# Hybrid decoder block: the cross-attention value weights of the prologue by column pairs, with transposes threaded in and the third token tile's statistics moved

## The reference

```python
k = (memn @ w_xk).reshape(B, M, XATTN_HEADS, XATTN_HEAD_DIM)
v = (memn @ w_xv).reshape(B, M, XATTN_HEADS, XATTN_HEAD_DIM)
s = jnp.einsum('bshd,bmhd->bhsm', q, k).astype(jnp.float32) * (XATTN_HEAD_DIM ** -0.5)
o = jnp.einsum('bhsm,bmhd->bshd', p, v).reshape(B, S, XATTN_HEADS * XATTN_HEAD_DIM)
```

## Time and profile before

| | |
|---|---|
| runs | 3040.64, 3043.88, 3046.34 us |
| median | 3043.88 us |
| the profiled execution, its own time | 3043.22 us |
| its span (first to last instruction) | 3041.5 us |
| TensorE busy | 2956.7 us |
| VectorE, ScalarE, GpSimd busy | 1627.4, 1069.0, 1255.0 us |

### The profile page before, as it was taken

The page is one execution under the profiler, slowest core; times in us unless marked ns, Lnnn a source line. Parts: engine busy times, 40 slices in busy tenths (PEclk is TensorE's granted clock), DMA queues, the critical chain, the costliest instruction groups (busy, mean ns, idle before and its releaser), DMA issues. The chain is left out here.

```text
span 3041.5 us, 41966 instructions
## 1 busy us (share of the span) xinstructions
PE 2956.7 (97%) x14334; PEld 2449.6 (81%) x14334; DVE 1627.4 (54%) x2236; ACT 1069.0 (35%) x1975; POOL 1255.0 (41%) x1126
## 2 busy tenths in 40 slices
PE   7999999999999999999999999999999999999998
PEld 7888788878878888878888778887888788887887
DVE  2564566645366444445565456665635644444445
ACT  4522445424233333322233244542423333332212
POOL 6422454452224444454442244445221444445433
PEclk9999999999999999999999999999999999999999
DMA  6622222141112222253322232224111122225221
GB/s 231 213 94 103 91 83 70 59 169 42 61 65 77 83 83 83 83 193 112 124 98 87 103 102 72 69 66 163 56 56 70 56 83 83 83 83 193 83 111 76
DMA packets 131685, 297.39 MB, mean 98 GB/s; under 512 B 11825, under 2 KB 52849, under 8 KB 131569
## 3 DMA queue, kind: packets, MB, share of 16 engines
q1 hardware_dynamic: 69072, 226.07, 21.4%
q10 hardware_dynamic: 62496, 69.78, 6.7%
HBM read 222.37 MB, written 73.43 MB: 97 GB/s over the span
## 5 line engine op out<-in xcount | busy, mean ns | idle before, releaser
L2409 DVE TENSOR_TENSOR h<-h,PS 128x1024 f32<-128x1024 f32 x272 | 330.9, 1220 | 332.0 <-PE PS L2588 214.9
L2586 PE MATMUL PS<-act_hi,w_hi 128*128 128x512 f32 (+1 forms) x1088 | 428.5, 394 | 9.5 <-issue 5.5
L1535 DVE TENSOR_TENSOR copied<-copied,PS 128x512 f32<-128x512 f32 x308 | 207.5, 685 | 400.9 <-PE PS L2588 387.9
L2588 PE MATMUL PS<-act_hi,w_lo 128*128 128x512 f32 (+1 forms) x1088 | 406.6, 374 | 0.0
L2587 PE MATMUL PS<-act_lo,w_hi 128*128 128x512 f32 (+1 forms) x1088 | 405.6, 373 | 0.0
L2050 POOL TENSOR_TENSOR w_lo<-raw,w_hi 128x256 fp32r<-128x256 f32 (+1 forms) x144 | 193.8, 1369 | 435.0 <-ACT w_hi L2127 435.0
L611 POOL TENSOR_TENSOR part_lo<-sum_s,part_hi 128x512 fp32r<-128x512 f32 x176 | 229.7, 1307 | 229.4 <-ACT part_hi L1060 229.4
L2586 PE MATMUL PS<-down,mid 128*128 128x512 f32 x704 | 276.6, 393 | 7.3 <-DVE h L2409 7.3
L2586 PE MATMUL PS<-op_t_hi,part_hi 128*128 128x512 f32 x704 | 275.3, 391 | 0.0
L2588 PE MATMUL PS<-down,mid 128*128 128x512 f32 x704 | 274.8, 390 | 0.0
L2587 PE MATMUL PS<-op_t_lo,part_hi 128*128 128x512 f32 x704 | 274.8, 390 | 0.0
(11 more groups left out here) (331 smaller groups left out, 6097.9 us busy)
## 6 DMA issues: line engine op xcount, KB each, us to landing
raw<-in_w_units SPq DMA_DIRECT2D x156, 512.0 KB, 3.9
gu_raw<-in_w_units SPq DMA_DIRECT2D x64, 512.0 KB, 5.1
a_d<-copied SPq DMA_DIRECT2D x88, 256.0 KB, 2.2
mid_raw<-a_d SPq DMA_DIRECT2D x44, 512.0 KB, 4.1
qkvz_d<-stage ACTq DMA_DIRECT2D x64, 256.0 KB, 2.7
raw<-att_d SPq DMA_DIRECT2D x32, 512.0 KB, 3.2
h<-in_x SPq DMA_DIRECT2D x12, 1024.0 KB, 7.9
prep_raw<-in_w_units SPq DMA_DIRECT2D x16, 512.0 KB, 4.4
```

Source lines behind the costliest of these rows:

```text
L1535: dve.tensor_tensor(buf[dst][:, :], buf[a][:, :], bank(k), ALU.add)\
L2409: dve.tensor_tensor(h[:, t, :], h[:, t, :], flat(bank(b + 2 * (t % 2), 2)), ALU.add)\
L2586: nc.tensor.matmul(out_ap, whi, xhi, start=start, stop=False)
L2588: return nc.tensor.matmul(out_ap, wlo, xhi, start=False, stop=stop)
```

## The change

The last two of the eight value tiles are no longer done tile by tile but pair of column blocks by pair: for each pair both tiles are added, so v0 is complete after the first 12 of the last 48 products. T0 is issued between the third and the fourth pair. The item table is reordered to v0 v1 v2 t0 v3 t1, on TensorE, ScalarE and VectorE. The first wait of the last two tiles is now for the last weight tile. Token tile 2's statistics go from ahead of v0 to behind p0 on ScalarE, its normalising from behind k7 to behind p1 on VectorE; tile 3's statistics go from behind p0 to behind p1, its normalising from behind p1 to behind t4. GpSimd's and SP's streams are not changed.

```diff
 PREP = {n: i for i, n in enumerate(
-    ["k%d" % u for u in range(KT)] + ["v%d" % q for q in range(KT // 2)] +
-    "t0 t1 t2 t3 p0 p1 t4 t5 p2 p3 t6 t7 p4 p5 p6 p7".split() +
+    ["k%d" % u for u in range(KT)] +
+    "v0 v1 v2 t0 v3 t1 t2 t3 p0 p1 t4 t5 p2 p3 t6 t7 p4 p5 p6 p7".split() +
     ["p%d" % i for i in range(8, 16)])}
 RING = 4
+PAIRED = 2
...
-X_TILE = dict(k7=[0, 1, 2], p1=[3], t5=[4], p3=[5], t7=[6], p5=[7])
-X_STATS = dict(p0=[3], t5=[4], p2=[5], t7=[6], p4=[7])
+X_TILE = dict(k7=[0, 1], p1=[2], t4=[3], t5=[4], p3=[5], t7=[6], p5=[7])
+X_STATS = dict(p0=[2], p1=[3], t5=[4], p2=[5], t7=[6], p4=[7])
...
-            for i in range(3):
+            for i in range(2):
                 x_stats(i)
-            for q in range(KT // 2):
-                prep_hi(act, f"v{q}")
-            for u in range(4):
-                prep_hi(act, f"t{u}")
+            for name in "v0 v1 v2 t0 v3 t1 t2 t3".split():
+                prep_hi(act, name)
...
-            for k in range(KT):
+            def value_weights(k, u):
+
                 n = KT + k
-                pe.wait_ge(S["w_lo_ready"], n + 1)
+                us = slice(u * P, (u + 1) * P)
+                return three(PS[:, u, 0:N_MEM], w_hi[n % RING][:, us], w_lo[n % RING][:, us],
+                             act_hi[:, k, 0:N_MEM], act_lo[:, k, 0:N_MEM], k == 0, k == KT - 1)
+
+            for k in range(KT - PAIRED):
+                pe.wait_ge(S["w_lo_ready"], KT + k + 1)
                 for u in range(KT):
...
+                    last = value_weights(k, u)
+                last.then_inc(S["vm_full"], 1)
+            pe.wait_ge(S["w_lo_ready"], 2 * KT)
+
+            def value_pair(q):
+
+                for u in (2 * q, 2 * q + 1):
+                    for k in range(KT - PAIRED, KT):
+                        last = value_weights(k, u)
+                last.then_inc(S["pr_full"], 1)
...
-            for u in range(4):
+            for q in range(3):
+                value_pair(q)
+            prep_transposes(0)
+            value_pair(3)
+            for u in range(1, 4):
                 prep_transposes(u)
```

More of the change, by code:

```diff
@@ L2748, in _ @@
             pe.wait_ge(S["pr_lo"], KT)
-            for k in range(KT):
+            def value_weights(k, u):
                 n = KT + k
-                pe.wait_ge(S["w_lo_ready"], n + 1)
-                for u in range(KT):
[L2753 to L2759, removed]
+                us = slice(u * P, (u + 1) * P)
[3 more added lines that the diff above has]
+                pe.wait_ge(S["w_lo_ready"], KT + k + 1)
+                for u in range(KT):
+                    last = value_weights(k, u)
[6 more added lines that the diff above has]
+                last.then_inc(S["pr_full"], 1)
             def prep_transposes(u):
```

## The result

The changed kernel takes 3047.46 us in the median of 20 runs (3045.07 to 3050.12), the kernel before 3042.11 in 20 (3039.56 to 3046.34): a ratio of 1.0018 with a 95% interval of 1.0011 to 1.0025. It is 5.3 us slower; the interval leaves 1 out, so the loss is real, but with 0.18% it lies just inside the 0.2% that the prediction had drawn as its line. The profiled execution of the changed kernel took 3048.43 us, its span 3046.7, 5.2 more than before.

A forecast was written before the change was run, and what follows sets the result against it. TensorE, busy for 97% of the span, was taken as the bound. The -1.2 us gain is inside +5.0; with +1.5 for the clock, +6.5 on 3043.22 gives 3049.7, 3050.4 for the runs, range 3045.0 to 3053.5.

The forecast's parts named there:

- The mechanism: GpSimd's third chain waits behind p0, delaying masks and fourth chain; VectorE waits at tile 3, TensorE at T7 5.2 us.
- Rival B: GpSimd's masks don't matter: T7 is not held if they take under 3.9 us; only the 1.2 us gain remains; chance 0.06.
- Pairs and freed queue: Last two value tiles by pairs, tile 2 out of VectorE's way: p0 at 76.14 instead of 77.36, a 1.2 us gain.
- The last weight tile: Start of value tile 6 on TensorE: its second half, ended by GpSimd at 64.52, is needed earlier; wait about 0.06 us.
- The tables: Moved statistics and normalising of token tiles on ScalarE and VectorE: no cost of their own forecast beside the masks.
- rival C: Low clock lasts through p4 into the tile transposes, and ScalarE's queue adds some: +7.4 to +9.5 us; chance 0.18.
- The masks: GpSimd's instructions between third and fourth chain: 9.16 us, from 82.62 to 91.8, making p4 5.0 us late.
- The clock: TensorE's clock falls to the low level after the 5.2 us hole at T7: 1.5 us, between 0 and 2.4.
- Rival A: T7 waits but the clock stays up, or the masks take 8.1 us: +5.0, or +4.0 to +5.5; chance 0.34.
- VectorE's wait: VectorE idle some 7.6 us until released by GpSimd's stat_r, named as a sign that the forecast is right.

The follow-up runs named there:

- masks first: The changed kernel with GpSimd doing two chains, then the masks, then the chains of tiles 2 to 7; 3041.71 us, ratio 0.9996 to the kernel before.
- p3 twice: The changed kernel with the 24 products of p3 issued twice into the same place; 3047.11 us, ratio 1.0017 to the kernel before.
- p3 three times: The changed kernel with the products of p3 issued three times into the same place; 3046.57 us, ratio 1.0017 to the kernel before.
- masks twice: The changed kernel with GpSimd's seven masks built twice; 3054.25 us, ratio 1.0042 to the kernel before.
- two masks behind: The changed kernel with five of seven masks ahead of GpSimd's third chain, two and the small rest behind it; 3042.09 us, ratio 0.9998 to the kernel before.

## Why the prediction came out as it did

The changed kernel was forecast at 3050.4 us in a range of 3045.0 to 3053.5; it took 3047.46. Of the 2.9 us between 3050.4 and that, 1.8 lie in the kernel before, whose median over 20 runs is 3042.11 and not the 3043.88 of three; the change itself was put at +6.5 and measured +5.3. The chances were split between slower (0.50) and within 0.2% (0.46), and the measured 0.18% falls into the second, close to the line.

**The mechanism** was right as put: GpSimd's unchanged order, the third chain in front of the masks, VectorE at tile 3, T7 behind t5. It is shown three ways, by taking it away, by doubling it and by finding where it starts. Rival B is out: the masks matter. Its threshold of 3.9 us was worked out from the time at which TensorE could take T7; 4.1 turned out free, since ScalarE's statistics hold the fourth chain as long anyway. That the two lie so close is luck.

**The terms**, from V to p8, +6.34 us:

- *Pairs and freed queue:* forecast -1.2, measured -1.27 with all weights in time (masks first). "What is late next is t1's split, 1.4": it was, 1.24.
- *The last weight tile:* forecast 0.06, measured 0.7. TensorE took tile 6 at 18.06 us after V in the changed kernel and at 17.37 in the masks-first one. The term was mis-sized since the low part's end, 64.52 in one trace, was taken for a fixed time. It hangs on a load. The lines are ScalarE's high part of the fourth value tile, before the change and after it, and GpSimd's last two low parts after it:

```profile
51.53 1.06 ACT L2189 ACTIVATE w_hi<-prep_raw 128x1024 fp32r<-128x1024 f32 x1 [2.79 <-DMA prep_raw<-in_w_units]
51.96 1.06 ACT L2190 ACTIVATE w_hi<-prep_raw 128x1024 fp32r<-128x1024 f32 x1 [2.77 <-DMA prep_raw<-in_w_units]
60.19 4.78 POOL L2029 TENSOR_TENSOR w_lo<-prep_raw,w_hi 128x1024 fp32r<-128x1024 f32 x2
```

  ScalarE waits for the load of this tile, in either kernel, and starts 4.39 us after V before the change and 5.00 after it. From there GpSimd makes five low parts without a pause, 2.4 us each, up to 64.97. The change asks for the last of them one tile, 2.9 us, earlier and so used up all the slack. Nothing in the change touches that load, so the term is not a fixed price: in the four kernels with the same program up to p0 this start lies from 4.19 to 5.00 us after V, and p0 scatters by 0.8 us. What delays the load is open.
- *The tables:* forecast nothing beside the masks, measured +1.3. The prediction saw that ScalarE has one statistics more between t5 and p2 and left it to rival C; it didn't ask what VectorE waits for once the masks are gone. This part of C was true.
- *The masks:* forecast 9.16, measured 91.68 - 83.05 = 8.63. They cost 35.86 - 30.28 = 5.58 from p0 to p8 with the clock, 4.2 without it. The 0.5 us that they are shorter is the first select, 1.10 us in place of 1.67. The forecast's 5.0 for p4 was net of the pairs' gain and had the tables' price in it unseen: without the gain it is 97.33 - 76.14 - (92.35 - 77.36) = 6.2 for masks and tables, measured 4.2 + 1.3 = 5.5.
- *The clock:* forecast 1.5, measured 1.35 (p4 alone 4.68 - 3.15 = 1.53). Rival A, that it would hold, is out: the fall is in the profiled execution, and the mean granted clock of a run is 0.995 in 17 of the changed kernel's 20 and 0.996 or 0.997 in all 11 of masks first. C's longer fall is out in the profiled execution: 16 of p4's 24 products start 0.21 us apart, the last 8 at 0.12. The row of the kernel's start that gave the upper 2.4 has the same 0.21, but the profile gives the granted clock there as 1.00, so it wasn't evidence of the low level by itself.

-1.27 + 0.7 + 1.3 + 4.2 + 1.35 = 6.3. That the forecast's 6.5 lies so near is in part luck: it had 0.7 too little for the weight tile and 0.7 too much for masks and tables.

**Why do the medians show 5.3?** The runs don't settle it. The interval of the ratio, 1.0011 to 1.0025, is 3.3 to 7.6 us and holds 6.3. One part that differs between executions is the weight tile's 0.7, which a typical run of the changed kernel need not pay in full. That the two profiled spans differ by 5.2 us and not by 6.3 has another reason: V comes 0.2 us earlier in the changed kernel's, and what lies behind p8 is 1.0 us shorter. From p8 to the end of the span the execution of the kernel before took 2935.2 us, that of the changed one 2934.2, the other ten 2932.0 to 2934.1, though nothing there was edited. A part of this may be the clock: summed over windows of 20 us, the granted clock is at the low level for 18 to 26 us behind p8, and not in the same places in every execution. A difference of two spans mixes this scatter in; the distances between p0 and p8 don't.

**What would show it:** T0 was forecast at 69.5 and came at 69.97, p0 at 76.1 and came at 76.62 (the late weight tile), the masks' start at 82.6 and came at 83.05. VectorE's wait was put at 7.6 and was 6.86, TensorE's at about 5 and was 4.24, and a slice at a granted 0.5 between 94 and 103 is there.

## What to carry to other kernels

When an item is moved on one engine, read the program of every engine that handles it: an in-order queue that wasn't edited still takes the item at its old place, and everything behind it waits along. Before threading work between engines, ask which single instruction the waiting engine is stuck on; here moving one VectorE instruction behind the urgent ones gave 1.25 us at p8, while the larger rearrangement lost 1.2 us without that and gained with it. And where a few microseconds are at stake, measure distances between fixed points of the trace rather than spans, in more than one execution where a load can be late.

## What the runs showed of the hardware that was not expected

- *The clock can fall though no idle stretch is long.* With p3 twice, dense products ran until 92.8; then came T6, 1.3 us of idle time, T7, 0.7 us of idle time, p4 at 96.9, and the clock fell near 97.1, already in p4. In the kernel before, T0 to T3 with 1.4 and 1.6 us of idle between 70.4 and 77.4 left it at the high level. What tells the two apart is open.
- *VectorE and GpSimd in each other's way, but not always to the end.* In the kernel before, VectorE's normalising began 0.13 us ahead of the first mask select, which took 1.67 us in place of 0.65. In the changed kernel it began 0.03 us ahead (83.26, 83.29); the select took 1.10 and ended before the normalising, which took 1.34 in place of 1.28. P3 twice, p3 three times, masks twice and two masks behind have the same: 0.02 or 0.03 us ahead, and 1.83 us for this select and the next together, as in the changed kernel.

```profile
L1977 POOL TENSOR_SCALAR_AFFINE_SELECT first_mask<-first_mask x2: 662/881/1100, 83.3 to 84.0; 128x64 f32<-128x64 f32 x2
```

  The Trainium skill, *SBUF — State Buffer*, section "Who interferes with whom", calls the port pair that VectorE and GpSimd share an exclusive lock and has the order of issue decide who blocks. The trace of before agrees: the select ends 0.5 us behind the normalising. The changed kernel's doesn't quite: by its row the loser's price was 0.45 us, against 1.02 before, for a tenth of a microsecond in the starts.
